# Recurrence of a hybrid trunk: two PE stages alternate with level products over two banks, and GpSimd forms part of the next chunk's operands

## The reference

```python
def rwkv_scan(s0, r, w, k, v, a_vec, b_vec, reverse, emit):
    def step(s, inp):
        r_t, w_t, k_t, v_t, a_t, b_t = inp
        sa = jnp.einsum('bhvk,bhk->bhv', s, a_t)
        s = s * w_t[:, :, None, :] + sa[..., None] * b_t[:, :, None, :] + v_t[..., None] * k_t[:, :, None, :]
        y = jnp.einsum('bhvk,bhk->bhv', s, r_t) if emit else None
        return s, y
```

## Time and profile before

| what | us |
|---|---|
| median of 3 runs | 2892.83 (2891.24 to 2895.13) |
| profiled execution, its own time | 2893.22 |
| its span | 2891.4 |
| PE busy | 2797.3 (97%) |
| DVE busy | 1185.1 (41%) |
| ACT busy | 683.0 (24%) |
| recurrence, six stretches in layer 0 | 137.10 |
| recurrence, six stretches in layer 1 | 132.80 |

### The profile page before, as it was taken

The page is one execution under the profiler, slowest core; times in us unless marked ns, Lnnn a source line. Parts: engine busy times, 40 slices in busy tenths (PEclk is TensorE's granted clock), DMA queues, the critical chain, the costliest instruction groups (busy, mean ns, idle before and its releaser), DMA issues.

```text
span 2891.4 us, 63725 instructions
## 1 busy us (share of the span) xinstructions
PE 2797.3 (97%) x29030; PEld 1683.3 (58%) x29030; DVE 1185.1 (41%) x2444; ACT 683.0 (24%) x1425; POOL 3.0 (0%) x7
## 2 busy tenths in 40 slices
PE   7999999999999999999999999989999999999997
PEld 4478777445777888864588787863333333333332
DVE  4777565445545444247786564431111011011101
ACT  2345312544322111013454126520000000000000
POOL 0000000000000000000000000000000000000000
PEclk9999999999999999999999999999999999999999
DMA  7100143212242433232000442459999999999995
GB/s 293 59 3 4 47 159 111 66 44 92 83 136 68 146 117 90 80 120 84 30 4 5 171 160 94 150 219 346 413 365 364 416 359 377 402 361 413 369 375 198
DMA packets 188787, 534.55 MB, mean 185 GB/s; under 512 B 6113, under 2 KB 80097, under 8 KB 171105
## 3 DMA queue, kind: packets, MB, share of 16 engines
q1 hardware_dynamic: 187440, 526.21, 48.6%
q0 software_dynamic: 1072, 4.19, 0.4%
HBM read 528.29 MB, written 2.10 MB: 183 GB/s over the span
## 4 chain that ended last, share of the span: by engine, by line
PE 92%; DVE 4%; ACT 1%; SPq 1%; issue 1%; DMA 1%; DVEq 0%; ACTq 0%
PE bank L572 68%; PE bank L700 12%; PE bank L1337 8%; PE bank L818 2%; PE bank L1199 1%; SPq L2990 1%; DVE WR L2456 1%; ACT ar L1627 0%; DMA rep<-in_repeated 0%; PE bank L923 0%; ACT WR L1627 0%; DVE RS L2330 0%; DVE AT L2127 0%; DVE ar L2389 0%; DVE WR L2437 0%
## 5 line engine op out<-in xcount | busy, mean ns | idle before, releaser
L572 PE MATMUL bank<-AT,WR 128*128 128x512 f32 (+1 forms) x1408 | 521.4, 521 | 5.9 <-ACT AT L1627 3.7
L1627 ACT ACTIVATE ar<-bank 128x256 f32<-128x256 f32 (+2 forms) x338 | 155.1, 463 | 1535.3 <-PE bank L572 1028.3
L572 PE MATMUL bank<-WR,ar 128*32 128x512 f32 (+1 forms) x4464 | 444.5, 555 | 1.6 <-DVE ar L2899 1.6
L572 PE MATMUL bank<-ar 128*32 128x512 f32 (+6 forms) x3990 | 429.6, 509 | 9.9 <-ACT ar L1627 5.9
L572 PEld LDWEIGHTS bank<-AT,WR 128*128 128x128 f32 x1408 | 263.0, 192 | 213.0 <-issue 196.9
L572 PEld LDWEIGHTS bank<-ar 128*32 128x32 f32 (+3 forms) x3990 | 176.1, 124 | 248.5 <-issue 237.3
L572 PEld LDWEIGHTS bank<-WR,ar 128*32 128x32 f32 x4464 | 143.7, 110 | 288.4 <-issue 285.8
L1627 ACT ACTIVATE WR<-bank 128x512 f32<-128x512 f32 (+1 forms) x224 | 122.8, 592 | 200.0 <-PE bank L572 174.7
L572 PE MATMUL bank<-AT,ar 128*32 128x512 f32 (+1 forms) x1456 | 151.5, 561 | 11.3 <-ACT AT L1627 11.3
L2909 DVE TENSOR_TENSOR YB<-YB,bank 128x512 f32<-128x512 f32 x28 | 18.0, 684 | 342.9 <-PE bank L572 342.9
L2917 DVE TENSOR_TENSOR ar<-ar,bank 128x512 f32<-128x512 f32 (+1 forms) x48 | 29.8, 621 | 286.9 <-PE bank L572 285.5
(11 more groups left out here) (368 smaller groups left out, 3287.6 us busy)
## 6 DMA issues: line engine op xcount, KB each, us to landing
WR<-in_moe_w_down SPq DMA_DIRECT2D x27, 2048.0 KB, 14.8
WR<-in_ada_w SPq DMA_DIRECT2D x20, 2048.0 KB, 8.0
ar<-in_moe_w_down SPq DMA_DIRECT2D x20, 2048.0 KB, 14.7
WR<-in_w_in SPq DMA_DIRECT2D x18, 2048.0 KB, 9.3
WR<-in_moe_w_gate SPq DMA_DIRECT2D x18, 2048.0 KB, 16.6
WR<-in_moe_w_up SPq DMA_DIRECT2D x15, 2048.0 KB, 15.9
WR<-in_moe_w_up SPq DMA_DIRECT2D x18, 1536.0 KB, 7.8
WR<-in_moe_w_gate SPq DMA_DIRECT2D x15, 1536.0 KB, 8.5
```

The lines of the kernel that those rows point to most:

```text
L572: return pe.matmul(o, lhsT, rhs, start=first, stop=last)
L1627: return act.activation(out, in_, func, **k)
```

## The change

On PE, from chunk 1 on, `solve(i - 1)` is no longer a stage of its own after level 0; its products alternate q by q with those of `level(i, 1)`. `values_turned(i)`, which was a stage after inverse 1, alternates with `level(i, 2)`. For that the solution goes to bank 2 and the turned values to bank 7 with both halves in one bank, and the last XT of a chunk gets a tile of its own (XT[2]).

The level products of a chunk go over two banks, d = 0 (q under 4) and d = 1, taken in turn from banks 0, 1 and 6 (`level_banks`, `grown_bank`, `turned_bank`), and DVE masks them in two instructions of 256 columns. The inverse's first half waits for the first, its second half for the second. Level 0 of a chunk waits, besides for inverse_ready, for the copy of the last chunk's G, and inverse 0 for the last copy of XT.

The four `against` pairs move back by one place each from chunk 1 on: they stood ahead of inverse 2, level 3, inverse 3 and level 4, and now stand ahead of level 3, inverse 3, level 4 and `from_state`; the bonus product stands ahead of inverse 2.

GpSimd forms the two rates, the responses and the centring for chunks 2 to 7. It waits for the exponentials and for the last chunk's G, and DVE's `operands` waits for its rates (rates_ready); the centring waits for operands_ready. On DVE these four instructions go, and `state`, `kept`, `begin_inverse` and `bonus_keys` stand in another order.

```diff
+        def level_banks(i, n):
+            return [banks[(0, 1, 6)[(5 * i + n + m) % 3]] for m in range(2)]
+
+        def grown_bank(i, n):
+            return banks[(0, 1, 6)[(5 * i + n + 2) % 3]]
+
+        def turned_bank(i, n):
+            return banks[(0, 1, 6)[(5 * i + n) % 3]]
+
+        solved_bank, gram_bank = banks[2], banks[7]
...
                     else:
                         pe.wait_ge(inverse_ready, seen(inverse_ready))
-                    S.done(("T1", l, i, n))
+                        if i:
+                            pe.wait_ge(A.free, A.jobs[("G", l, i - 1)])
+                    if beside == "solve":
+                        pe.wait_ge(A.free, A.jobs[("XT", l, i - 1, 4)])
...
                     for q in range(8):
+                        bank = level_banks(i, n)[q // 4]
                         for h in range(2):
-                            ins = mm(pair(level_bank, q, 1 - h if n else h), pair(LTs[i % 2], q, h),
-                                     pair(X[n > 0], q, h), True, True)
-                            if (q, h) == (7, 1):
-                                ins.then_inc(S.full, 1)
-                        if beside:
-                            for h in range(2):
+                            ins = mm(pair(bank, q, 1 - h if n else h), pair(LTs[i % 2], q, h), pair(X[n > 0], q, h), True, True)
+                        if q % 4 == 3:
+                            ins.then_inc(S.full, 1)
+                            S.done(("T1", l, i, n, q // 4))
+                        for h in range(2 if beside else 0):
+                            if beside == "solve":
+                                solve(i - 1, q, h)
+                            elif beside == "values":
+                                value_turned(i, q, h)
+                            else:
                                 last = gram(i + 1, beside, gram_bank, q, h)
...
                     if i:
                         level(i, 0)
-                        solve(i - 1)
                         inverse_doubled(i, 0)
+                        level(i, 1, "solve")
+                        inverse_doubled(i, 1)
                         y_of_chunk(i - 1, ybank)
-                        level(i, 1)
                         state(i - 1)
-                        inverse_doubled(i, 1)
-                        values_turned(i)
+                        level(i, 2, "values")
                         if i <= 4:
                             bonus(i - 1)
-                        level(i, 2)
+                        inverse_doubled(i, 2)
                         pe.wait_ge(responses_ready, seen(responses_ready))
                         against(i, 0)
-                        inverse_doubled(i, 2)
-                        against(i, 2)
                     level(i, 3, "X" if i < NCH - 1 else None)
-                    against(i, 4)
+                    against(i, 2 if i else 4)
                     inverse_doubled(i, 3)
-                    against(i, 6)
+                    against(i, 4 if i else 6)
                     level(i, 4, "LT" if i < NCH - 1 else None)
...
-                def masked(n):
-                    TT(dq(T1), step_product(banks[6]), mk(M_LEVEL + 1 + n), ALU.mult).then_inc(S.free, 1)
+                def masked(i, n):
+                    for d in range(2):
+                        bank = level_banks(i, n)[d]
+                        TT(dq(T1)[:, d], step_product(bank)[:, d],
+                           masks[:, M_LEVEL + 1 + n, d, :].unsqueeze(1).to_broadcast([128, 4, CH]), ALU.mult).then_inc(S.free, 1)
...
                         if i < NCH - 1:
-                            dve.wait_ge(A.full, A.jobs[("G", l, i - 1)])
-                            rates_in(l, i + 1)
+                            dve.wait_ge(rates_ready, 2 * (NCH - 2) * l + 2 * i)
                             operands(l, i + 1)
-                        masked(1)
+                        masked(i, 1)
...
+            def recurrence(l):
+                rows = Rc.rearrange("p d j c w -> p d j (c w)")
+                for i in range(1, NCH - 1):
+                    b = (i + 1) % 2
+                    pool.wait_ge(decayed, 2 * NCH * l + 2 * i + 4)
+                    pool.wait_ge(A.full, A.jobs[("G", l, i - 1)])
+                    TT(per_d(BK[b][:, :, 0:64]), both(Rkk, i + 1), by_direction(Ra, i + 1, CH), ALU.mult).then_inc(rates_ready, 1)
+                    TT(per_d(BK[b][:, :, 64:128]), both(Rk, i + 1), key_rate, ALU.mult).then_inc(rates_ready, 1)
+                    TT(per_d(per_q(MV[:, b, 1, :])), both(Rr, i + 1), per_d(per_q(E1)), ALU.mult).then_inc(responses_ready, 1)
+                    if i + 2 < NCH:
+                        pool.wait_ge(operands_ready, NCH * l + i + 2)
+                        middle = by_direction(rows, i + 2, CW, 32, 1)
+                        TT(CC.rearrange("p (d j) w -> p d j w", d=2), by_direction(rows, i + 2, CW, 0, CW),
+                           middle.to_broadcast([128, 2, 4, CW]), ALU.subtract).then_inc(centred, 1)
```

162 lines of the change are left out of this document (89 added, 73 removed).

## The result

| | before | changed |
|---|---|---|
| median, us | 2892.71 (2891.24 to 2895.13) | 2911.01 (2909.86 to 2913.54) |
| span of the profiled execution | 2891.4 | 2907.8 |
| recurrence, six stretches of layer 0 | 137.1 | 145.7 |
| recurrence, six stretches of layer 1 | 132.8 | 138.0 |

The ratio is 1.0063, 95% interval 1.0050 to 1.0075: 18 us slower, outside the range of the forecast. Of the 16.4 us in the span 13.8 lie in the twelve stretches. The page of the changed kernel answers the earlier trace rows: the same number of products, the same number of instruction packets, 12 us less PE work, and POOL at work.

The account below looks back on a forecast made before the run. Instruction fetch was taken as the bound beside PE: a 264.6 us floor plus 2 us of new waits gave 266.6 against 269.9, −3.3 us, so 2889.5 us. The range ran from 2871 to 2904.

Parts of the forecast that it names:

- The floor: Instruction fetch on PE in both recurrences: 3.78 us per 256 instructions, 70 blocks, 264.6 us against 269.9 used.
- rival 1: Fetch stops are no floor and the chain rules: late chunks 19.6 us, sum −24.4, 2868.5 us; chance 0.17.
- (a, b): Solution product alternating with level 1, turned values with level 2: each gives back 1.08 us per chunk, 26 us of PE.
- rival 3: Alternating products do not run side by side, so nothing is gained: 2893 us; chance 0.06.
- (c): Level products over two banks, masked in halves: inverse may start at 1.19 instead of 1.94 us after its level began.
- The walk along the chain: Steps of a late chunk from level 0 to the next level, with PE waiting for the chain: 19.6 us.
- every block is shorter than 3.78: The chain cut into blocks of 256 PE rows: 2.8 to 3.5 us each, so the stops grow by what is freed.
- The price of a pass: One POOL pass: taken as 1.4 us, between 0.68 and 3.35, at no cost.
- the rates would not be late: POOL's two rates ahead of DVE's operands: they fit if each takes at most 1.33 us.
- up to D = 1.8 costs nothing: D is one rate's time on POOL; beyond 1.33 us the block has 1.0 us of room below the floor.
- rival 2: POOL late: 2902 us at D = 2.3; or DVE and POOL holding each other up at bonus_in and operands: +16; chance 0.22.
- The signs that the forecast named: Profile after: late chunks 22 to 23 us, PE busy 1.5 to 2 less, stops in nearly all blocks, DVE 2.4 less.

Follow-up runs that it names:

- e1: Changed kernel with the GpSimd part undone (rates, responses, centring back on DVE), all of the PE part kept: 1.0039, 11.3 us over the kernel before.
- e5: Kernel before with only level products over two banks, masks in halves and both solution halves in one bank: 1.0016, 4.6 us over before.
- e4: e1 with each level product in one bank and masked whole, in one instruction: 1.0102, 29.5 us over the kernel before.
- e10: Changed kernel with GpSimd's responses formed only after DVE's operands: 1.0055, 15.9 us over the kernel before.
- e15: Changed kernel with 32 extra products at the program's start, moving instruction block borders by 128: 1.0055, 15.9 us over the kernel before.
- e16: Changed kernel with 16 extra products at the program's start, moving instruction block borders by 64: 1.0049, 14.2 us over the kernel before.
- e2: Kernel before with only the GpSimd part (rates, responses, centring on POOL): 1.0023, 6.7 us over before.
- e8: e5 plus solution alternating with level 1 and turned values with level 2, against pairs in their old places: 1.0032, 9.3 us over the kernel before.
- e11: e10 with the two rates back on DVE, POOL forming only responses and centring: 1.0031, 9.0 us over the kernel before.
- e12: e9 with responses and centring on POOL, both behind operands: 0.9997, −0.9 us against the kernel before.
- e18: e10 with bonus_in moved behind masked(1) and POOL's responses after it, so bonus_in meets no POOL pass: 1.0021, 6.1 us over the kernel before.
- e6: e5 plus the solution product alternating with level 1, output and state products behind inverse 1: 1.0056, 16.2 us over the kernel before.
- e7: e5 plus the turned values alternating with level 2: 1.0002, 0.6 us over the kernel before.
- e9: e7 with the solution's halves in two banks again, a copy behind each: 0.9996, −1.2 us against the kernel before.
- e13: e1 plus 16 unused products between inverse 0 and level 1 in each of 14 chunks: 1.0069, 20.0 us over the kernel before.
- e14: Kernel before with 32 extra products at the program's start, moving instruction block borders by 128: 1.0010, 2.9 us over before.
- e17: Kernel before plus unused products ending layer 0's recurrence, without waits, then six early or late per block: 3.96 us per block with waits, either way.
- e3: Kernel before plus three runs of 512 unused products that wait for nothing (64, 96, 128 columns), ending layer 0's recurrence: 2980.2 us in one run.

## Why the prediction was wrong

**What bounds the kernel now.** The floor exists: 3.78 us read from the trace, 3.74 (once 3.47) measured alone. Its sum was wrong. It multiplied 3.78 by 70 blocks, as if each took that. The 18 blocks it rested on were chosen by ending in a stop. All 68 blocks of the steady part of the kernel before come to 263.03 us, a mean of 3.87, and among them are seven of 4.72 to 5.18 us, six of these with PE at work throughout, like the first here:

```profile
192.02:197.20 5.18, 5.18 (x126) 3.98 (x126) 2.98 (x6) 1.92 (x4) 0.00 (x0) 1.00 0.02 3
```

What such a block has over 3.78 is not given back by the next one: behind these seven stand blocks of 3.61 to 4.89 us. Nor is 3.78 a floor for every block: nine of the 68 took 2.99 to 3.40, one of them 3.04 behind one of 4.20; rival 1 rested on the shortest. How far a block can fall below it, and behind what, no run measured. In the changed kernel the 68 blocks come to 276.94 us, 4.07 each, and those that are long hold waits, not work (the first, and the sum):

```profile
181.12:187.56 6.44, 3.83 (x126) 3.59 (x128) 5.94 (x8) 2.46 (x8) 4.74 (x3) 1.00 0.01 3
...
sum 276.94, PE 234.05 PEld 200.54 DVE 197.51 ACT 144.61 POOL 63.50; mean PE 3.44 PEld 2.95 DVE 2.90 ACT 2.13 POOL 0.93
```

**What the change takes off PE (a, b).** Forecast 26 us, measured 16.7 in e1 (237.4 against 254.1 us busy). The mechanism was right, though 9 of the 26 us did not come, for which no cause was found; and rival 3 is out: where nothing interrupted it, level 2 with the values was through in 0.93 us (e1, 288.41 to 289.34), as a bare level.

**(c) Halves.** As a term of its own it showed no gain: with the old order DVE's masks ended hardly a wait, and e5 was 4.6 us slower, part of it by the solution's one bank. Once the covering stages are gone it is worth 18 us (e4 against e1).

**What waits in its place.** The walk along the chain was right step by step up to the first stop (inverse 0 at 1.38 for a forecast 1.19, level 1 at 3.22 for 3.05, in e1). Behind it every step came later: in that chunk the output product at 6.84 for 5.37, level 4 at 18.7 for 14.6, the next level 0 at 23.9 for 19.6. Three stops are 2.0 of these 4.3 us; the other 2.2 lie in the steps themselves, 0.5 each at the output product and at level 4, both behind waits for ACT's copies. **The step that failed is the conclusion from it, "every block is shorter than 3.78", so that the waits cost nothing.** In its place the runs showed that stops and waits add up, since they fall into different blocks: 4.07 us per block in the changed kernel, and in e1 12.8 us more waiting for ACT, 7.0 for masks and 4.8 in stops, against 16.7 of work saved. The late chunks of e1 took 24.3 and 23.2 us in layer 0 and 22.6 and 23.6 in layer 1, where 22 to 23 was forecast. Cost of the PE part: 11.3 us, where −3.3 was forecast for the whole change.

**What moves to GpSimd.** The price of a pass, taken at 1.4 us between 0.68 and 3.35, was right (1.27 alone, 1.55 on average with holds), and so was that the rates would not be late: DVE waited 1.1 us for them in layer 0. **The second failed step is "up to D = 1.8 costs nothing".** It counted only lateness and put the hold into rival 2, against a room of 1.0 us below the floor. The hold is real: 1.7 us of DVE time per chunk, and nearly half of it falls on bonus_in, which had no room at all, since masked(0) stands right behind it. Rival 2 gave +16 by this mechanism and named bonus_in and operands as the places; operands was the harmless one. It had a chance of 0.22 and was over a third of what happened (6.9 us of 18). That its +16 lies near the measured 18 is luck: it had the PE part gain 3 us, and that part cost 11.

**The signs that the forecast named.** POOL passes of 1.1 to 1.8 us: yes. DVE busy 2.4 us less per chunk: no, 0.5 (202.7 against 208.3 in twelve), the rest was standing still. PE busy 1.5 to 2 us less per late chunk: 0.8, and 1.0 in e1 (20.3 and 20.1 for 21.1). Stops at nearly every border: no, at 42 of 70 PE's next instruction came more than 0.19 us late, at 35 of 70 before.

## What to carry to other kernels

A stage that looks like pure cost on the busiest engine may be the cover of a wait: before it is merged into another, write down which wait stood beside it, and price it without cover. A floor per block of instructions is not an average to multiply by: lay the blocks along the program, count for each the larger of the floor and its own length with its waits, and don't take the mean from those alone that show the stop. Work for GpSimd that reads SBUF belongs beside vector operations that read PSUM; next to operations with two SBUF inputs it stops them for a whole pass, and the pass with a critical operation behind it is where that is paid.

## What the hardware showed unasked

TensorE's granted clock fell to its lower level, 1.2 GHz, inside the recurrence of the changed kernel, which it never did in the steady part before. A window from 1.6 us after PE's wait of 2.6 us in layer 0, and the one behind it:

```profile
188.90:192.30 3.40, 3.20 (x128) 3.18 (x128) 1.51 (x3) 1.71 (x4) 1.07 (x1) 0.58 0.00 0
192.30:196.00 3.70, 3.65 (x136) 3.32 (x130) 1.25 (x4) 1.20 (x3) 0.00 (x0) 1.00 0.02 4
```

There a product took 0.32 us instead of 0.22 to 0.23. It happened three times in the twelve stretches of the changed kernel (near 189, 1462 and 1486), three times in e10, twice in e4, e15 and e16, once each in e1, e2, e8, e11, e12 and e18, and not in e5, e6, e7, e9, e13 and e14; each kernel has one profile. Two of the three stand behind a wait of 2.6 us; the third behind waits of 0.7, 1.0 and 0.7, and the one of e1 (near 308) behind 0.7 and a stop of 1.1. In e17 the clock was low from 378 to 395, behind 14 us in which PE had been busy for 8.4; in e3 the same blocks ran from 358 to 376, as little busy, at the upper level throughout. So these rows give no rule for when it falls. Blocks of e17 with six waits took 6.18 us at the lower level instead of 3.96.

So idle time of PE can cost twice. How much of the 18 us this is was not measured by itself. An estimate from the rows: a level of 64 rows took 1.65 us (189.10 to 190.75) instead of 0.93, so PE loses 1.1 to 1.5 us each time, at most 4 us in the changed kernel; and the block around the first (187.56 to 191.33) took 3.77 us, no more than one that only waits for instructions, so part of it is covered. Of the 12.1 us between the changed kernel and e18 two such times, at most 3 us, can be the clock.
